# The order of 256-column and 512-column matmuls inside each product of a split-precision MLP, on one Trainium2 core

## The reference

```
h2 = rmsnorm(x, norm_ffn)
g = causal_dwconv(h2 @ ffn_w_gate, ffn_conv_w)
x = x + (silu(g) * (h2 @ ffn_w_up)) @ ffn_w_down
```

## Time and profile before

| | |
|---|---|
| median of 3 runs | 2108.95 us (2108.43 to 2110.01) |
| the profiled execution's own time | 2111.68 us |
| its span, first to last instruction | 2109.8 us |
| PE busy | 2101.2 us (100% of the span), 11304 matmuls |
| DVE / ACT / POOL busy | 1557.5 (74%) / 1000.6 (47%) / 1274.9 us (60%) |
| DMA | 146 GB/s over the span |
| granted TensorE clock | 1.0 (2.4 GHz) in every slice |

### The profile page before, as it was taken

How to read it: one execution, slowest core, us unless ns; L and a number is a source line. 1 busy time by engine, 2 the same in 40 slices (tenths; PEclk the granted TensorE clock), 3 DMA queues, 4 the chain that set the end, 5 groups by cost and what they waited for, 6 DMA issues and landing times.

```text
span 2109.8 us, 34285 instructions
## 1 busy us (share of the span) xinstructions
PE 2101.2 (100%) x11304; PEld 1774.8 (84%) x11304; DVE 1557.5 (74%) x2794; ACT 1000.6 (47%) x1459; POOL 1274.9 (60%) x732
## 2 busy tenths in 40 slices
PE   9999999999999999999999999999999999999999
PEld 7778777887888888888888888888888888888888
DVE  6487465457663226888888888888888799988987
ACT  6334344434433446445546545555555554444543
POOL 5345334444544656667767767767767676666665
PEclk9999999999999999999999999999999999999999
DMA  6224223233333444344444544544544766655743
GB/s 211 84 78 124 64 68 98 95 106 102 103 100 125 144 146 135 133 167 135 161 162 135 170 158 138 171 153 142 171 145 145 244 220 205 223 186 186 235 154 132
DMA packets 150117, 308.74 MB, mean 146 GB/s; under 512 B 13272, under 2 KB 54424, under 8 KB 149880
## 3 DMA queue, kind: packets, MB, share of 16 engines
q1 hardware_dynamic: 103568, 250.39, 35.9%
q10 hardware_dynamic: 46440, 56.94, 8.6%
HBM read 261.64 MB, written 45.51 MB: 146 GB/s over the span
## 4 chain that ended last, share of the span: by engine, by line
PE 97%; DVE 2%; DMA 1%; issue 0%; SPq 0%; ACT 0%; ACTq 0%
PE ps L889 40%; PE ps L888 21%; PE ps L690 11%; PE ps L694 11%; PE ps L691 11%; PE ps L755 0%; PE ps L781 0%; PE ps L795 0%; PE ps L767 0%; PE ps L836 0%; DMA comb<-act_lo 0%; DMA resid<-xT 0%; PE ps L822 0%; PE ps L839 0%; DVE resid L1508 0%
## 5 line engine op out<-in xcount | busy, mean ns | idle before, releaser
L889 PE MATMUL ps<-comb,fhi 128*128 128x512 f32 x3507 | 1234.2, 394 | 0.0
L888 PE MATMUL ps<-comb,flo 128*128 128x256 f32 x3507 | 985.1, 281 | 0.0
L889 PEld LDWEIGHTS ps<-comb,fhi 128*128 128x128 f32 x3507 | 657.3, 187 | 149.2
L634 POOL TENSOR_TENSOR flo<-raw,fhi 128x1024 fp32r<-128x1024 f32 (+2 forms) x252 | 484.7, 1935 | 359.8 <-ACT fhi L1229 359.0
L888 PEld LDWEIGHTS ps<-comb,flo 128*128 128x128 f32 x3507 | 662.4, 189 | 6.1 <-DVE ps L1854 2.1
L604 POOL TENSOR_TENSOR wlo<-raw,whi 128x512 fp32r<-128x512 f32 x260 | 360.1, 1398 | 395.1 <-ACT whi L1007 344.1
L634 POOL TENSOR_TENSOR flo<-sum,fhi 128x1024 fp32r<-128x1024 f32 (+2 forms) x168 | 323.7, 1932 | 39.2 <-ACT fhi L1229 39.1
L1229 ACT ACTIVATE fhi<-ps 128x1024 fp32r<-128x1024 f32 (+2 forms) x168 | 141.7, 844 | 420.1 <-DVE ps L1728 240.9
L690 PE MATMUL ps<-hhi,whi 128*128 128x512 f32 x784 | 316.7, 404 | 1.5 <-POOL wlo L604 1.1
L694 PE MATMUL ps<-hlo,whi 128*128 128x512 f32 x784 | 306.6, 391 | 0.1
L691 PE MATMUL ps<-hhi,wlo 128*128 128x512 f32 x784 | 305.7, 390 | 0.0
(11 more groups left out here) (252 smaller groups left out, 2622.8 us busy)
## 6 DMA issues: line engine op xcount, KB each, us to landing
raw<-w_gu SPq DMA_DIRECT2D x176, 512.0 KB, 3.7
raw<-w_in SPq DMA_DIRECT2D x196, 256.0 KB, 3.2
raw<-w_dn SPq DMA_DIRECT2D x96, 256.0 KB, 2.8
raw<-w_dn SPq DMA_DIRECT2D x64, 320.0 KB, 3.1
act_hi<-pair_sums ACTq DMA_DIRECT2D x20, 896.0 KB, 4.2
act_lo<-pair_sums ACTq DMA_DIRECT2D x20, 896.0 KB, 8.2
raw<-w_out SPq DMA_DIRECT2D x64, 256.0 KB, 3.2
comb<-act_hi SPq DMA_DIRECT2D x21, 512.0 KB, 3.9
```

The lines of the kernel that those rows point to most:

```text
L634: nc.gpsimd.tensor_tensor(flo[s][:, 0:w], src[:, 0:w], fhi[s][:, 0:w].bitcast(F32), ALU.subtract).then_inc(f_lo_pool, 1)
L888: nc.tensor.matmul(dst[:, 0:HT], flo[s][:, w], both[:, HI, :], start=fresh and k == 0, stop=False, skip_group_check=True)
L889: ins = nc.tensor.matmul(dst, fhi[s][:, w], both, start=False, stop=k == n - 1, skip_group_check=True)
```

## The change

Inside a product of a merged unit all low-weight matmuls (256 columns) come first, for k = 0 to n-1, then all high-weight ones (512 columns). The very first product of unit 0 (which has `before`) and the products of unit 44 keep their order. Numbers, operands and banks of the matmuls are the same, so are all waits and increments.

```diff
@@ -878,6 +878,19 @@
 
                 b, s, n = ACTS[pos], slot(u, pos), width(u) // P
                 half = 0 if gate_up(u) else 4 * ((u - FT) // NPAIR % 2)
+
+                def both(k):
+                    return pair_sums[:, b] if apart(u, k) else block_of(b)[:, :, half + k, :]
+
+                if merged(u) and before is None:
+
+                    for k in range(n):
+                        nc.tensor.matmul(dst[:, 0:HT], flo[s][:, k * P:(k + 1) * P], both(k)[:, HI, :],
+                                         start=fresh and k == 0, stop=False, skip_group_check=True)
+                    for k in range(n):
+                        ins = nc.tensor.matmul(dst, fhi[s][:, k * P:(k + 1) * P], both(k), start=False, stop=k == n - 1, skip_group_check=True)
+                    ins.then_inc(f_used, 1)
+                    return
                 for k in range(n):
                     if before is not None:
                         before(k)
```

## The result

On the chip of the first comparison the changed kernel took 2113.02 us (median of 12 runs, 2111.5 to 2115.28), the kernel before 2109.2 us (12 runs, 2106.2 to 2113.86): a ratio of 1.0017, with a 95% interval from 1.0009 to 1.0024. A gain of 7 us was forecast; a loss of 4 us was measured, which is itself at the edge of what can be told from no change.

What follows compares the result with a forecast made beforehand. The prediction took PE's distance between matmul starts to bound the kernel. Slow beat -10 us and entries +3 made -7, so 2104.7 us for the profiled execution and 2102 us set against the median, range 2097 to 2116.

Steps and rivals of the forecast that it cites:

- What bounds the kernel: Claim that PE carries 97% of the chain, with a single 0.5 us wait in the MLP and clock 1.00.
- The slow beat: MLP pairs at 0.3533 us instead of 0.3467, set in behind pauses; the runs were to remove it, -10 us.
- The settled runs: Inside runs, narrow matmuls start 0.120 us apart and wide ones 0.2267, together the quick pair's 0.3467.
- I take +0.005: Net cost in us assumed per product for entering its wide and narrow runs; over 580 products +3 us.
- the dense row: The wide matmul behind unit 44, next start after 0.24 us against 0.23, read as an entry of +0.01 us.
- the longer kind: Worse wide-run entry seen behind small matmuls: seven wide ones take 1.63 us against 1.587 settled, +0.043 us.
- The gain of the narrow entries: First narrow matmuls of a run start quicker than settled: up to -0.02 us a product, half taken, -0.01.
- The pauses: Loop pauses in gate/up, 2 us, stay; at most 3 us more, left out of the sum, kept for the range.
- Every product pays an entry: Rival: each of 580 narrow-to-wide switches disturbs PE, 20 us less 10, giving 2119 us; chance 0.20.
- the shorter kind of entry: Wide-run entry of +0.026 us, from five wide matmuls behind small ones; over 580 products it gave 2114 us.
- Order is indifferent: Rival: the slow beat is set by pauses and carries on in runs, so time stays 2109 us; chance 0.30.
- The rule beside it: Start gap is columns by 2.4 GHz plus 2.5 ns whatever the neighbours, so the reordering is worth 0 us.

Runs made afterwards that it cites:

- one_per_unit: Only product 1 of each unit in a narrow run then a wide run, all others in pairs as in the kernel before: 2119.59 us, ratio 1.0032.
- all_narrow: Each wide matmul of the kernel before split in two of 256 columns, its weights loaded twice: 2148.82 us.
- wide_first: Every reordered product with its wide run first, then its narrow run: 2113.61 us, ratio 1.0004 to the kernel before.
- snake: Changed kernel with neighbouring products mirrored so that their runs join: 2109.33 us, ratio 0.9985 to the kernel before.
- before_a: The unchanged kernel before, run again with its own profile: 2113.26 us, ratio 1.0003 to the same program beside it.
- before_b: The unchanged kernel before, one more execution with its own profile: 2113.68 us in that execution.
- fours: In gate/up four narrow, four wide, four narrow, four wide, down as in the changed kernel: 2116.8 us, ratio 1.0019 to the kernel before.

## Why the prediction was wrong

- **What bounds the kernel**: right. PE's chain, its single wait and the clock stayed as they were.
- **The slow beat, -10 us**: right in size (10.3 us of pace in that profile) and in that the runs do away with it: nothing of the pattern of rows 6 is left, and narrow matmuls stand at 120 ns. Its description was half right. "It sets in behind a pause" and "holds until the next" are true of the loop, but one_per_unit showed that it is the rule behind settled runs, and in the down units of four blocks the beat changes every few us with no pause at all, as between 1933 and 1942 us of the profile before, where no start is more than 15 ns late. The 10 us are moreover those of an execution 2.7 us above the median, and they were taken off the median; how many slow pairs the median execution had no profile shows.
- **The settled runs, 0.120 and 0.2267 us**: right; all_narrow and the sixth to eighth wide matmul of each run stand there.
- **"I take +0.005" for both entries together**: this is the step that failed. Measured 0.020 us in a product of 8 or 5 blocks and 0.015 in one of 4: 11 us over 580 products in place of 3. The bounds (-0.02 and +0.043) held. The mistake was to go by the dense row, the first wide matmul behind unit 44, with its +0.01: it shows only the first of what are five late starts in a run. The row from the w_in stage, five wide matmuls with +0.026, had the whole sequence, and it was set aside because it stood behind small matmuls. It has nearly the same shape and size as the entries behind narrow runs: 230, 236, 229, 232 and 231 ns, +0.025 by the exact starts, against +0.0275. By them the longer kind is +0.038, not +0.043.
- **The gain of the narrow entries**: -0.01 assumed, half of what nine matmuls of unit 44 show, -0.0075 measured in a run of 8; nearly right.
- **The pauses**: "30 x 0.1 = 3 us at most" was put into the range. A loop pause shows about 0.085 us at a narrow matmul after the change; the stops rose from 4.1 to 5.3 us, nearly all of it the wait in unit 44, which varies from profile to profile (0.3 to 1.8 us), in the unchanged kernel too (0.3, 0.5 and 1.4).
- **The rival "Every product pays an entry"** named the mechanism, its place and its count; with the shorter kind of entry it gave 2114 us, and 2113.0 was measured. It was given 0.20 where it should have led, as one row spoke for its size and none for a smaller one over a whole run.
- **"Order is indifferent"** (2109 us) came within 4 us of the time, for a wrong reason and by luck: two costs of the order happened to be about equal. The rule beside it (the Trainium skill, "TensorE: Matmul & The Clock Gate", Back-to-back issue gap: columns by the clock plus 2.5 ns, given for a matmul apart from its weight load, with no term for the neighbours) fits the form of the traces where the neighbours have the same width, with 13 ns in place of 2.5. It doesn't hold where widths change: 580 against 290 passages made 4.3 us between wide_first and snake.

What it is in the hardware that makes the first five wide matmuls late is not shown. The record rules out two things: it is no wait (none in the list), and no matter of the boundary between products (wide_first). That weight loads hold PE up is spoken against, but not ruled out for mixed widths: with a load every 120 ns all_narrow loses nothing.

## What to carry to other kernels

A PE that is busy all the time still has a pace, and it shows only in the distances between starts: compare them with the settled distance for that width, over a whole sequence and not at its first member. Here changes of width cost some 20 ns a passage into a long run and 0 to 7 ns in alternation; equal widths cost nothing, and where widths must differ, mirror neighbouring groups so that runs join (worth 0.2% here). When a kernel has two beats and chance picks between them, take many runs on more than one chip before you call 0.2% a difference.

## What the runs showed that was not expected

A pace can be bistable: the same pair of instructions takes 0.3467 or 0.3533 us for tens of us on end, with widths of 256 and 512 as with 320 and 448. From 2009 us to the end the kernel before has only quick pairs in the profile ahead of the prediction and only slow ones in before_a and before_b.

The loop of gate/up shows a pause every 39 us in all variants but all_narrow, which issues half as many matmuls more and has none of them: 3336 matmuls in 400 us, twice.

In the profiled execution of fours, PE stood still for about 2 us in unit 44 and ran on for some 1.5 us before its clock fell. The timeline of PE across the wait, then the stretches behind it (columns as in rows 4, for all of PE's matmuls):

```profile
1686.18 0.28 PE L915 MATMUL ps<-pair_sums,fhi 128*128 128x256 f32 x1
1688.21 0.39 PE L913 MATMUL ps<-comb,fhi 128*128 128x256 f32 x1 [1.76 <-DMA comb<-act_lo]
...
1690.61 1.48 PE L895 MATMUL ps<-comb,fhi 128*128 128x512 f32 x3
1691.89 0.63 PE L895 MATMUL ps<-pair_sums,fhi 128*128 128x512 f32 x1
```

```profile
1688.30:1689.80 1.50, 1.50 (x13) 0.97 1.06 400
1689.80:1693.10 3.30, 3.30 (x13) 0.50 0.32 121
1693.10:1696.00 2.90, 2.90 (x19) 1.00 0.24 59
```

The granted clock is 0.50 (1.2 GHz) for 3.3 us, although PE is dense there; the starts there are 213 ns (256 columns) and 427 ns (512, 1.28 us for three above) apart in place of 120 and 227, about 1.5 us lost. This is 256 and 512 columns by 1.2 GHz to the nanosecond, while at full clock the settled distances are 13 ns over the columns: at the low clock neither this surcharge nor an entry shows. In no other profile of this study did the clock fall at that place. The 7.0 us of stops of fours contain this loss.
